# An FFN's up map by block products in 2x2 form (seven instead of eight), with the residual stream parked in DRAM

## The reference

```
z = h @ w_up                     # 1024 -> 6144
u, v = z[..., :D_FF], z[..., D_FF:]
u = dwconv(u, conv_w, conv_b)    # 3 taps along the tokens
y = (gelu(u) * v) @ w_down       # 3072 -> 1024
x = x + g_f * rms_norm(y, norm_post_ffn)
```

## Time and profile before

| | us |
|---|---|
| median of 3 runs (2322.86 to 2323.80) | 2323.55 |
| the profiled execution | 2322.84 |
| its span, first to last instruction | 2321.1 |
| TensorE busy | 2197.9 |
| VectorE busy | 1235.6 |
| GpSimd busy | 818.8 |
| ScalarE busy | 727.8 |

### The profile page before, as it was taken

How to read it: one execution, slowest core, us unless ns; L and a number is a source line. 1 busy time by engine, 2 the same in 40 slices (tenths; PEclk the granted TensorE clock), 3 DMA queues, 4 the chain that set the end, 5 groups by cost and what they waited for, 6 DMA issues and landing times.

```text
span 2321.1 us, 25336 instructions
## 1 busy us (share of the span) xinstructions
PE 2197.9 (95%) x9592; PEld 1773.2 (76%) x9592; DVE 1235.6 (53%) x1155; ACT 727.8 (31%) x810; POOL 818.8 (35%) x414
## 2 busy tenths in 40 slices
PE   7899996969999999999999979799999999999996
PEld 7677774857888888888888768578888888888885
DVE  6688986076544544554554584743443344344436
ACT  3567565233221222212122344422222122212222
POOL 1423324355343343343434362432223222332223
PEclk9999998969999999999999979799999999999998
DMA  6133231202122122212212200011111111111101
GB/s 263 68 113 108 72 113 56 108 19 82 63 85 84 67 80 81 81 63 81 81 63 90 73 19 19 10 64 45 45 45 50 50 45 45 45 45 45 54 27 73
DMA packets 43413, 158.12 MB, mean 68 GB/s; under 512 B 4304, under 2 KB 4592, under 8 KB 42224
## 3 DMA queue, kind: packets, MB, share of 16 engines
q1 hardware_dynamic: 43376, 157.63, 19.5%
HBM read 153.42 MB, written 4.19 MB: 68 GB/s over the span
## 4 chain that ended last, share of the span: by engine, by line
PE 84%; ACT 6%; DVE 5%; issue 2%; POOL 2%; ACTq 0%; DMA 0%; POOLq 0%; DVEq 0%
PE ps L366 75%; PE ps L498 3%; PE ps L699 1%; PE ps L405 1%; DVE acc L1196 1%; ACT TH L843 1%; PE ps L441 1%; DVE Y L1289 1%; DVE Y L1276 1%; PE ps L666 1%; POOL X L1042 1%; PE ps L687 1%; PE ps L463 1%; ACT RA L849 1%; ACT H_hi L779 1%
## 5 line engine op out<-in xcount | busy, mean ns | idle before, releaser
L1493 DVE TENSOR_TENSOR Y<-Y,ps 128x1024 f32<-128x1024 f32 x336 | 410.3, 1221 | 538.0 <-PE ps L366 538.0
L366 PE MATMUL ps<-H_hi,WA_hi 128*128 128x512 f32 x960 | 315.1, 405 | 29.0 <-DVE H_lo L1282 11.4
L366 PE MATMUL ps<-H_hi,WB_hi 128*128 128x512 f32 x960 | 307.9, 397 | 5.1 <-ACT Y L855 3.5
L366 PE MATMUL ps<-H_lo,WA_hi 128*128 128x512 f32 x960 | 309.1, 399 | 0.0
L366 PE MATMUL ps<-H_hi,WA_lo 128*128 128x512 f32 x960 | 308.5, 398 | 0.0
L1002 POOL TENSOR_TENSOR WA_lo<-rawA,WA_hi 128x1024 fp32r<-128x1024 f32 x60 | 145.9, 2432 | 456.7 <-ACT WA_hi L733 456.7
L366 PE MATMUL ps<-H_hi,WB_lo 128*128 128x512 f32 x960 | 306.7, 396 | 0.0
L366 PE MATMUL ps<-H_lo,WB_hi 128*128 128x512 f32 x960 | 306.6, 396 | 0.0
L1002 POOL TENSOR_TENSOR WC_lo<-rawC,WC_hi 128x1024 fp32r<-128x1024 f32 x46 | 110.2, 2396 | 417.7 <-ACT WC_hi L741 417.7
L366 PEld LDWEIGHTS ps<-H_hi,WA_hi 128*128 128x128 f32 x960 | 177.1, 190 | 76.9 <-issue 27.7
L366 PE MATMUL ps<-F_hi,WC_hi 128*128 128x512 f32 x736 | 234.7, 396 | 0.6 <-DVE M L1259 0.6
(11 more groups left out here) (203 smaller groups left out, 3022.2 us busy)
## 6 DMA issues: line engine op xcount, KB each, us to landing
rawA<-wA SPq DMA_DIRECT2D x60, 512.0 KB, 3.3
rawB<-wB SPq DMA_DIRECT2D x60, 512.0 KB, 3.3
E<-ada SPq DMA_DIRECT2D x48, 512.0 KB, 3.8
rawC<-wC SPq DMA_DIRECT2D x48, 512.0 KB, 4.4
quad<-ada SPq DMA_DIRECT2D x8, 2048.0 KB, 9.6
ada_first<-ada SPq DMA_DIRECT2D x4, 2048.0 KB, 16.4
Y<-xT SPq DMA_DIRECT2D x4, 1024.0 KB, 22.4
X<-xT SPq DMA_DIRECT2D x4, 1024.0 KB, 6.4
```

What stands on the lines that cost most here:

```text
L366: mm = pe.matmul(out, w[:, w_cols:w_cols + P], (hi, lo)[part], start=first and w is W_hi[s] and part == 0, stop=last and w is W_lo[s])
L1493: TT(Y[:, m], Y[:, m], flat(ps[:, b:b + 2, :]), ALU.add).then_inc(d_added, 1)
```

## The change

Steps 1 to 23 of each FFN make u and v of both halves from seven block products instead of eight (step 0 stays as it was). The blocks are: of the weights A1, A2 (u, input tiles 0 to 3 and 4 to 7) and B1, B2 (v); of the input H11, H21 (first half of the tokens, input tiles 0 to 3 and 4 to 7) and H12, H22 (second half). Once in each FFN, T1 = H12 - H11, T3 = H22 - H12, T2 = T3 + H11 and T4 = T2 - H21 are made by VectorE (`right_raws`, 16 half-width instructions, each with its high part on ScalarE and low part on VectorE, T4's on GpSimd). For each step GpSimd makes S1 = B1 + B2, S2 = S1 - A1, S3 = A1 - B1 and S4 = A2 - S2 (`combine`). TensorE does "11" = A1 H11, "12" = A2 H21, "S4" = S4 H22, "S1" = S1 T1, "S2" = S2 T2, "S3" = S3 T3 and "22" = B2 T4: 12 matmuls each, into one bank each (`quarter`). VectorE adds: u0 = P11 + P12, u2 = P11 + PS2, u1 = u2 + PS1 + PS4 (two adds), u3 = u2 + PS3, v1 = u3 + PS1, v0 = u3 - P22; u0, u1 are the halves of u, v0, v1 of v. The combination S_i lies in the low part's place, so it waits until the step's product S_i is done.

`down(L, j-1)` now follows the seven products. There is one ada buffer E instead of two (E_first serves unit 1 only). The T blocks take X's place: X is stored to DRAM before an FFN (`save_x`, eight DMAs of 512 KB) and loaded again after the last product S3 (`reload_x`). The loads of C wait for the end of the down map before; those of A and B for the combinations and low parts. The buffers of the pooling stage move to other addresses, and its loads are reordered. The parts of the diff that matter here (`p["12"]` and the like are the banks of OUT; `copy_p1` copies P11 to t1 on ScalarE; `taps` is L1522 and L1525 with the adding of v0 between them; `gated` is the product with v, from SBUF now, except in step 0):

```diff
+        OPS = {"11": (W_hi["A"], W_lo["A"], 0), "12": (W_hi["A"], W_lo["A"], HF),
+               "S3": (W_hi["B"], W_lo["B"], 0), "22": (W_hi["B"], W_lo["B"], HF),
+               "S1": (So_hi, So_lo, 0), "S2": (So_hi, So_lo, HF), "S4": (So_hi, So_lo, 2 * HF)}
...
+        PE_ORDER = ("11", "12", "S4", "S1", "S2", "S3", "22")
+        READY_ORDER = ("11", "12", "S1", "S2", "S4", "S3", "22")
+        READY_FIRST = ("S1", "11", "12", "S4", "S2", "S3", "22")
+        MADE_ORDER = ("S1", "S2", "S3", "S4")
...
+        OUT = {"11": 2, "12": 3, "S4": 6, "S1": 7, "S2": 2, "S3": 3, "22": 2}
...
+            def load_unit(e):
+                if isinstance(e, int) and e < 2:
+                    sp_.wait_ge(ada_out, NH + 1)
+                else:
+                    sp_.wait_ge(red_made, 4 * NH + e)
+                dst, full = (E_first, e1_full) if isinstance(e, int) and e == 1 else (E, e_full)
+                sp_.dma_start(dst[:], ada[48 + e].rearrange("p (k m) -> p k m", k=KT)).then_inc(full, 16)
...
+            def save_x(i):
+                for h in range(2):
+                    for q in range(4):
+                        wait_new(sp_, i, h, 2 * q)
+                        wait_new(sp_, i, h, 2 * q + 1)
+                        sp_.dma_start(outT[:, 2 * q:2 * q + 2, hs(h)], X[:, 2 * q:2 * q + 2, hs(h)])\
+                           .then_inc(x_saved[q // 2], 16)
+            def reload_x(L):
+                for q in range(2):
+                    sp_.wait_ge(x_saved[q], 64 * (L + 1))
+                sp_.wait_ge(op_done, done_at("S3", UP * (L + 1)))
+                for h in range(2):
+                    for q in range(4):
+                        sp_.dma_start(X[:, 2 * q:2 * q + 2, hs(h)], outT[:, 2 * q:2 * q + 2, hs(h)])\
+                           .then_inc((x_full, res_full)[h][q], 16)
+            def load_up(L, j):
+                n = N_STD + FJ * L + j
+                sp_.wait_ge(made, made_at("S4", UP * L + j - 1))
+                if isinstance(j, int) and j == 2:
+                    sp_.wait_ge(op_ready, ready_at("12", UP * L + 1, True))
+                sp_.dma_start(raw["A"][:], wA[n]).then_inc(raw_full["A"], 16)
+                sp_.wait_ge(op_ready, ready_at("22", UP * L + j - 1))
+                sp_.dma_start(raw["B"][:], wB[n]).then_inc(raw_full["B"], 16)
+            def load_down(L, j):
+                sp_.wait_ge(d_done, 8 * (FJ * L + j))
+                sp_.dma_start(raw["C"][:], wC[FJ * L + j]).then_inc(raw_full["C"], 16)
...
             def ffn_loads(L, j):
...
+                if not (isinstance(j, int) and j == 1):
+                    load_down(L, j - 1)
+                if L == 0:
+                    load_unit(2 * j)
+                    load_unit(2 * j + 1)
+                if not (isinstance(j, int) and j > FJ - 3):
+                    load_up(L, j + 2)
...
                 for m in range(KT):
                     if m < 2:
-                        if not (isinstance(c, int) and c == 0):
-                            pe.wait_ge(d_added, 8 * c)
-                        if m == 0 and L == 0:
-                            pe.wait_ge(ada_added, NH + 2 + j)
+                        if not first:
+                            pe.wait_ge(d_added, 8 * c + m - 1)
+                        if m == 1 and L == 0:
+                            pe.wait_ge(ada_added, NH + 3 + j)
                     elif m == 2:
-                        pe.wait_ge(u_evac, c + 2)
+                        pe.wait_ge(up_added, added_at("v1", t + 1))
                     else:
                         pe.wait_ge(d_added, 8 * c + m - 2)
-                    b = (4, 6, 0)[m % 3]
+                    b = (4, 0, 6)[m % 3]
...
+                first, last = static and j == 1, static and j == FJ - 1
+                if not (first and L == 0):
+                    pe.wait_ge(up_added, added_at("v0", t - 1))
+                quarter("11", t, first)
+                quarter("12", t, first)
+                if not first:
+                    pe.wait_ge(d_added, 8 * c - 10)
+                quarter("S4", t, first)
+                quarter("S1", t, first)
+                pe.wait_ge(t1_made, t)
+                quarter("S2", t, first)
+                if first and L == 0:
+                    pe.wait_ge(u_evac, 1)
+                    pe.wait_ge(cols_full, 16)
+                    pe.matmul(ps[:, 0, 8:8 + 4 * KT], cnt_row[0:4 * KT], ident[0:4 * KT, 0:4 * KT],
+                              start=True, stop=True).then_inc(cols_made, 1)
+                    ada_columns(4 * NH + 2, 2, ps[:, 0, 0:2])
+                pe.wait_ge(up_added, added_at("u0", t))
+                quarter("S3", t, first)
+                pe.wait_ge(up_added, added_at("u2", t))
+                quarter("22", t, first)
+                if L == 0:
+                    if first:
+                        pe.wait_ge(ada_added, NH + 2)
+                    else:
+                        pe.wait_ge(d_added, 8 * (c - 1))
+                    ada_columns(4 * NH + 2 * j + 2, 2, ps[:, 0, 0:2])
+                if not last:
+                    down(L, j - 1)
...
+            def ffn_first(L):
+                round_t(L, 0)
+                round_op("S1", L, 1)
+                round_op("11", L, 1)
+                round_op("12", L, 1)
+                if L:
+                    act.wait_ge(conv_done, FJ)
+                A(Ub[:, 1:T + 1], flat(AB01), ACT.Copy).then_inc(u_evac, 1)
+                act.wait_ge(u_evac, L + 1)
+                tap(L, 0)
+                round_op("S4", L, 1)
+                round_t(L, 2)
+                round_t(L, 1)
+                round_op("S2", L, 1)
+                round_op("S3", L, 1)
+                round_op("22", L, 1)
+                round_t(L, 3)
+                copy_p1(UP * L + 1)
+                gelu(L, 0)
...
+                act.wait_ge(f_mul, t)
+                A(F_hi[:], S[1][:], ACT.Copy).then_inc(f_hi, 1)
+                if not first:
+                    copy_p1(t)
+                if not (first and L == 0):
+                    round_down(L, j - 1)
+                if not last:
+                    round_op("11", L, j + 1)
+                    round_op("12", L, j + 1)
+                    round_op("S1", L, j + 1)
...
+                act.wait_ge(up_added, added_at("u1", t))
+                act.wait_ge(f_mul, t)
+                tap(L, j)
+                if not last:
+                    round_op("S2", L, j + 1)
+                    round_op("S4", L, j + 1)
+                    round_op("S3", L, j + 1)
+                gelu(L, j)
...
+            def ffn_first(L):
+                for name in ("S1", "S2", "S3", "S4"):
+                    combine(name, L, 1)
+                for name in ("S1", "11", "12", "S4", "S2", "S3", "22"):
+                    lo_of_op(name, L, 1)
+                for k in range(KT // 2):
+                    pool.wait_ge(t_hi, 16 * L + 12 + k + 1)
+                    TT(T_lo[3][:, k], T_raw[3][:, k], T_hi[3][:, k].bitcast(F32), ALU.subtract)\
+                        .then_inc(t4_lo, 1)
...
-                if not last:
-                    lo_of_unit("A", n + 1)
+                first, last = static and j == 1, static and j == FJ - 1
...
+                    ada_product(2 * j)
+                pool.wait_ge(f_hi, t)
+                TT((F_lo_last if last else F_lo)[:], S[1][:], F_hi[:].bitcast(F32), ALU.subtract)\
+                    .then_inc(f_ready, 1)
+                if not (first and L == 0):
+                    lo_of_unit("C", t - 1)
                 if last:
...
+                    if L == 0:
+                        ada_product(2 * j + 1)
+                    pool.wait_ge(lastw_hi, L + 1)
+                    TT(W_lo["A"][:], raw["B"][:], W_hi["A"][:].bitcast(F32), ALU.subtract)\
+                        .then_inc(lastw_ready, 1)
                     return
...
+                lo_of_op("11", L, j + 1)
+                lo_of_op("12", L, j + 1)
+                if L == 0:
+                    ada_product(2 * j + 1)
+                for name in ("S1", "S2", "S3", "S4"):
+                    combine(name, L, j + 1)
+                for name in ("S1", "S2", "S4", "S3", "22"):
+                    lo_of_op(name, L, j + 1)
...
+            ada_product(0)
+            ada_product(1)
             next_stream(1, 0, lambda h: fill_ffn(0, h))
...
+            def ffn_first(L):
+                right_raws(L)
+                right_lo(L, 1)
+                taps(L, 0)
+                right_lo(L, 2)
                 if L == 0:
...
+                    ada_sum(0, 0)
+                    ada_sum(0, 1)
...
+                gated(L, j - 1)
+                if L == 0 and not first:
+                    ada_sum(j, 0)
+                dve.wait_ge(op_done, done_at("12", t))
+                dve.wait_ge(t1_made, t)
+                TT(u_0, t1[:], p["12"], ALU.add).then_inc(up_added, 1)
                 if L == 0:
...
+                    if first:
+                        dve.wait_ge(cols_made, 1)
```

(48 more changed lines are left out.)

458 lines of the change are left out of this document (273 added, 185 removed).

## The result

The changed kernel takes 2367.57 us (median of 4 runs, 2364.94 to 2371.26), the kernel before 2323.2 beside it (4 runs, 2320.88 to 2323.8): ratio 1.0194, 95% interval 1.0176 to 1.0212. It is 1.9% slower; the prediction said 2371, with a range of 2318 to 2400. The execution profiled takes 2371.26 with a span of 2369.5, 48.4 us more than the profiled execution of before.

A forecast was written before the change was run, and what follows sets the result against it. TensorE's matmuls were taken to bound the kernel. In us, 2.5 + 36.1 + 35.7 + 0.5 + 25.4 - 50.2 - 1.5 = +48.5 on 2322.84 gave 2371, range 2318 to 2400.

The forecast's parts named there:

- Bound before, and what is removed: Both FFNs: time is matmul count times 0.2333 us spacing; 132 instead of 144 a step removes 128.8 us.
- FFN 1's step: FFN 1's loop: 31.2 us against 33.59, with a 0.4 stall at down tile 3; -50.2 over 21 steps.
- FFN 0's step: FFN 0's loop: 35.75 us against 34.05, stalls of 1.6 before product 22 and 2.5 before down tile 1; +35.7.
- the clock: FFN 0's steps: slow 1.2 GHz matmuls behind the second stall cost 0 to 1.2 us a step; a quarter taken.
- Rival (b): The clock falls in each step of FFN 0: +0.9 x 21, kernel 2390 us; chance 17%.
- First steps: Half-width VectorE and GpSimd work in turns leaves TensorE idle: +36.1 us in FFN 0, +25.4 in FFN 1.
- 20 less without turns: Lower bound for each first step's added time: 20 us less if VectorE and GpSimd take no turns.
- Operand waits: VectorE instructions reading two SBUF operands and GpSimd instructions wait for each other's whole; taps near 2 us instead of 1.28.
- Parking: Storing and reloading X costs nothing, covered by matmuls, norm and step 0; at half bandwidth 11 us late.
- Ends and the ada products ahead: FFN ends: +0.5 us in FFN 0, -1.5 in FFN 1; ada products of units 0 and 1 before FFN 0: +2.5.
- (a): Loop steps' waits do not bind: steps 31.25 and 30.8 us, kernel 2267, or 2287 if only operand waits vanish; 14% together.
- (d): Half the first steps' loss and FFN 0's step at 35.1: -25 - 13.6, kernel 2332 us; chance 9%.

The follow-up runs named there:

- e8: e7 plus, in first steps, ScalarE's tap of step 1 ahead of rounding S1, and in FFN 0 unit 3's sum and the bias between the taps; 2260.98 us.
- e1: Changed kernel, but in FFN 0's loop steps VectorE sums ada unit 2j+1 behind u1's two adds instead of ahead of the add u2; 2324.73 us.
- e2: Changed kernel, but in FFN 0's loop steps VectorE adds the ada columns' bias behind v0, between the taps, instead of behind the second; 2332.76 us.
- e5: Changed kernel, but in both FFNs' loop steps GpSimd waits for VectorE's second tap before low parts of S1, S2, S4, S3, 22; 2338.39 us.
- e4: Changed kernel, but down tiles use PSUM banks 4, 6, 0 in turn instead of 4, 0, 6, waits moved with them; 2336.33 us.
- e3: Changed kernel with both moves: sum of ada unit 2j+1 behind u1, and the ada columns' bias between the taps; 2280.71 us.
- e10: e9 plus, in both FFNs' loop steps only, GpSimd's five last low parts wait for VectorE's second tap; 2262.26 us.
- e11: e7 plus, in each FFN's first step, GpSimd makes low parts of S3, 22 and T4 only behind VectorE's low parts of T3; 2271.25 us.
- e7: e3 plus, in FFN 0's first step, VectorE sums ada units 0 and 1 behind T1's low parts instead of T3's; 2270.03 us.
- e6: Kernel before, with only the storing and reloading of X (the residual stream) added; 2323.75 us against 2323.79.
- e9: e8 with the down tiles' bank order 4, 6, 0 of e4 added; 2260.38 us.

## Why the prediction was right, and where it was not

**Bound before, and what is removed: right.** FFN 1 shows the removal clean: 132 matmuls, 30.77 us a step, no wait that a row shows. The spacing of a single matmul to a bank is 0.2333 as read from the earlier trace rows. That 132 x 0.2333 is 30.8 is in part luck: 48 of the 132 stand closer, and a small wait makes up for it (see FFN 1's step). By rows the removal is worth 128.8 us, and e8 keeps 63 of it. The Trainium skill ("TensorE: Matmul & The Clock Gate", Part 1) gives 215.7 ns between matmuls of 512 columns; no trace here bears that out: where matmuls of 512 columns follow each other at the full clock, they stand 233 or 227 ns apart.

**FFN 0's step: right in mechanism, one term short.** Both waits at the places forecast, each shown by its own move (e1, e2), and each by VectorE's order, not its load. Sizes: the first wait is 2.08 instead of 1.6, since the ada unit was in use 0.8 later than the landing of the earlier trace rows had it. The second is 1.67 instead of 2.5: the longer first wait and the slow matmuls behind it bring the end of tile 0 to 24.6 us into the step (forecast 23.1), the bias ends at 26.2 (25.5). Each costs some 0.27 beyond its figure: idle time counts from a matmul's modelled end, 0.40 behind its start, where the next would have started after 0.23, and the first one behind it is 0.1 slow (849.01 to 849.35). Slow matmuls, 109 of them in the 21 steps, cost 1.03 a step on average. So 36.38 is 30.93 (84 x 0.2333, 48 x 0.2267, 0.45 of columns) + 3.75 + 0.54 + 1.03, and 0.13 left over. The term that failed is the clock: "the price is 0 to 1.2 a step; I take a quarter", 0.3. It rests on one gap of the earlier trace rows, and nothing there says how often it happens; and it was put behind the second wait alone, where 9 of the 15 runs stand behind the first. Rival (b), the clock down in each step, was nearer in this term; its 2390 failed because FFN 1 was better than forecast. How often: in 14 of 20 steps with waits of 2.1 and 1.7 us, in 9 with one of 2.4 (e1), in 6 with 2.0 and 1.0 (e5), in 5 and 10 with 2.1 and 0.5 (e2, e4; why these two differ is not known), in none with 0.7 (e3) or 0.9 (e10).

**FFN 1's step: the stall is there but smaller, and the down matmuls are closer than priced.** At 23.8 us into the step, where tile 3 begins, two starts are 0.34 apart, too short a gap to be shown as idle. e5, whose shorter taps let the first down add come earlier, takes it away: 30.51 for 30.77, so it is 0.26 where the forecast had 0.4. The other 0.3 is the 48 down matmuls at 0.2267 instead of 0.2333 (last section). Together 0.43 x 21 = 9 us. The step of 30.77 lies outside the 31 to 31.5 that the prediction named as its sign.

**First steps: right, +35.2 and +22.7 against +36.1 and +25.4.** The idle time was where it was put: in FFN 0 ahead of product 11, of the columns of units 0 and 1, of 22, and of the columns of units 2 and 3:

```profile
546.70 0.79 PE L709 MATMUL ps<-H_hi,WA_hi 128*128 128x512 f32 x1 [5.54 <-POOL WA_lo L1330]
...
575.24 0.58 PE L494 MATMUL ps<-ones,red 128*128 128x1 f32 x2 [10.17 <-DVE red L1479]
...
584.63 0.50 PE L709 MATMUL ps<-H_hi,WB_hi 128*128 128x512 f32 x1 [2.17 <-DVE U L1863]
...
598.31 0.34 PE L494 MATMUL ps<-ones,red 128*128 128x1 f32 x1 [10.62 <-DVE red L1479]
```

The turns of half-width instructions are shown by e11 (3.48 for four, where e7 has 6.7). The bound "20 less without turns" was wrong as a bound for the time: taking turns away on one engine leaves the other's queue.

**Operand waits: right.** e5 takes them away and both sides return to their own time. The Trainium skill ("SBUF — State Buffer", the shared port pair) has it that whichever of the two starts first keeps that pair for its whole instruction; e5's return from 1.82 to 1.28 and from 1.94 to 1.30 agrees.

**Parking: right**, nothing (e6). **Ends and the ada products ahead: right** to 1 us each.

**Rivals.** (a) did not happen in the kernel as changed, but order alone comes near it: e7 to e9 get FFN 0's step to 31.8 (31.25 in (a)), and the best stand at 2261, though with shorter first steps, which (a)'s 2267 did not have. (d) fell, since the first steps lost what was forecast; its 25 for half the entry loss is also too little, half of 36.1 + 25.4 being 30.8.

## What to carry to other kernels

When a change takes work from the bounding engine and gives it to two others, put the new instructions in the order in which the bounding engine needs their results, and look first for a result that stands behind an instruction which waits for a slow chain: two such places cost 87 us of 2368 here, twice what the kernel then gains on the one before, with neither engine over 70% busy in that loop. Count a wait of 2 us on TensorE at more than its length, and where one wait goes, look at once for what that step wants next (e9). A forecast that agrees in the sum may still hold two errors: compare it stage by stage.
